# Diffusion-trunk step on one Trainium2 core: score matmuls of a head's two maps issued in turn, pass by pass

## The reference

```python
def diff_attention(q, k, v, lam):
    ...
        s = jnp.einsum('bqhsd,bkhsd->bshqk', qblk.astype(jnp.float32), kf) * scale
        p = jax.nn.softmax(s, axis=-1)
        a = p[:, 0] - lam * p[:, 1]
        return jnp.einsum('bhqk,bkhv->bqhv', a, vf)
```

## Time and profile before

| | |
|---|---|
| median of 3 runs | 2035.17 us (2033.72 to 2036.74) |
| span of the profiled execution | 2036.0 us |
| PE busy | 1926.5 us, 95% of the span |
| DVE busy | 1603.3 us, 79% |
| ACT busy | 1164.4 us, 57% |
| attention stage | about 524 to 720 us of the span |
| DMA queue q1, packet time | 68.5% of 16 engines over the span |

### The profile page before, as it was taken

How to read it: one execution, slowest core, us unless ns; L and a number is a source line. 1 busy time by engine, 2 the same in 40 slices (tenths; PEclk the granted TensorE clock), 3 DMA queues, 4 the chain that set the end, 5 groups by cost and what they waited for, 6 DMA issues and landing times.

```text
span 2036.0 us, 25353 instructions
## 1 busy us (share of the span) xinstructions
PE 1926.5 (95%) x9008; PEld 1373.6 (67%) x9008; DVE 1603.3 (79%) x1588; ACT 1164.4 (57%) x1190; POOL 151.9 (7%) x130
## 2 busy tenths in 40 slices
PE   4899999999789887799999999999999999999998
PEld 2787777877677766566666666666666666666665
DVE  4599437333577756679999999999999999999997
ACT  5444324232477722167667666767676776766764
POOL 0265203000011110000000000000000000000000
PEclk8899999999799998799999999999999999999999
DMA  8233634433222120299999999999999999999996
GB/s 295 99 114 140 232 125 134 159 115 124 79 63 82 44 94 31 102 319 366 343 352 354 348 347 347 357 339 347 354 347 347 347 355 344 350 350 342 351 355 219
DMA packets 270387, 504.50 MB, mean 248 GB/s; under 512 B 11372, under 2 KB 37268, under 8 KB 270328
## 3 DMA queue, kind: packets, MB, share of 16 engines
q1 hardware_dynamic: 266648, 491.10, 68.5%
q0 software_dynamic: 3680, 12.60, 1.7%
HBM read 486.86 MB, written 16.80 MB: 247 GB/s over the span
## 4 chain that ended last, share of the span: by engine, by line
PE 83%; DVE 6%; POOL 3%; DMA 2%; ACT 2%; SPq 2%; issue 1%; DVEq 0%; ACTq 0%; POOLq 0%
PE banks L1454 23%; PE banks L1456 23%; PE banks L1455 23%; PE banks L1730 2%; PE banks L1616 2%; PE banks L1731 2%; POOL qk_swp L1381 2%; POOL qk_swp L1376 1%; DMA v_h<-v_scr 1%; PE banks L1473 1%; PE banks L1474 1%; DVE w_lo L912 1%; PE banks L1588 1%; PE banks L1718 1%; PE banks L1701 1%
## 5 line engine op out<-in xcount | busy, mean ns | idle before, releaser
L1342 DVE TENSOR_TENSOR w_lo<-raw,w_hi 128x2048 fp32r<-128x2048 f32 x285 | 649.9, 2285 | 71.2 <-ACT w_hi L889 70.3
L889 ACT ACTIVATE w_hi<-raw 128x2048 fp32r<-128x2048 f32 x285 | 546.0, 1916 | 129.4 <-PE banks L1456 113.9
L1454 PE MATMUL banks<-w_hi,xe_hi 128*80 128x512 f32 x1024 | 404.9, 395 | 2.6 <-issue 2.6
L1456 PE MATMUL banks<-w_lo,xe_hi 128*80 128x512 f32 x1024 | 402.9, 393 | 0.0
L1455 PE MATMUL banks<-w_hi,xe_lo 128*80 128x512 f32 x1024 | 402.4, 393 | 0.0
L889 ACT ACTIVATE w_hi<-raw_x 128x2048 fp32r<-128x2048 f32 x96 | 184.3, 1920 | 153.7 <-PE banks L1456 106.5
L1454 PE MATMUL banks<-w_hi,h_hi 128*128 128x512 f32 x560 | 223.5, 399 | 2.0 <-POOL h_lo L1368 1.0
L1342 DVE TENSOR_TENSOR w_lo<-raw_x,w_hi 128x2048 fp32r<-128x2048 f32 x96 | 218.9, 2280 | 5.4 <-ACT w_hi L889 5.3
L1455 PE MATMUL banks<-w_hi,h_lo 128*128 128x512 f32 x560 | 221.7, 396 | 0.0
L1456 PE MATMUL banks<-w_lo,h_hi 128*128 128x512 f32 x560 | 221.7, 396 | 0.0
L1456 PEld LDWEIGHTS banks<-w_lo,xe_hi 128*80 128x80 f32 x1024 | 151.2, 148 | 85.1 <-issue 0.5
(11 more groups left out here) (208 smaller groups left out, 2505.4 us busy)
## 6 DMA issues: line engine op xcount, KB each, us to landing
raw<-in_w_gate_e SPq DMA_DIRECT2D x128, 1024.0 KB, 5.1
raw<-in_w_down_e SPq DMA_DIRECT2D x96, 1024.0 KB, 5.1
raw<-in_w_up_e SPq DMA_DIRECT2D x64, 1024.0 KB, 5.5
raw_x<-in_w_up_e SPq DMA_DIRECT2D x64, 1024.0 KB, 5.4
raw_x<-in_w_down_e SPq DMA_DIRECT2D x32, 1024.0 KB, 5.2
raw<-in_w_in SPq DMA_DIRECT2D x28, 1024.0 KB, 5.6
raw<-in_w_ada SPq DMA_DIRECT2D x24, 1024.0 KB, 5.9
raw<-in_w_out SPq DMA_DIRECT2D x4, 1024.0 KB, 5.3
```

The costliest lines, as they stand in the source:

```text
L889: nc.scalar.activation(w_hi[:, j % NSPLIT], raw_slot(slot), ACT.Copy).then_inc(hi_done, 1)
L1342: nc.vector.tensor_tensor(w_lo[:, j % NSPLIT], raw_slot(EXPERT_SLOT[j % NRAWE]), w_hi[:, j % NSPLIT], ALU.subtract).then_inc(lo_done, 1)
L1454: nc.tensor.matmul(ps, hi, wh, start=first, stop=False)
L1456: return nc.tensor.matmul(ps, hi, wl, start=False, stop=last)
```

## The change

The waits for both maps now stand ahead of the first score matmul of a unit. The matmuls are issued pass by pass: high by high of map 0, then of map 1, low by high of map 0, then of map 1, and so on, at 512 columns and then at 256. The number, shapes, operands and banks of the matmuls are the same. Each map's `sc_done` is raised by its own last matmul. No other engine's program changes. The score matmuls have line L1608 now, and `weigh` L1620.

```diff
                 for s in range(2):
                     if u >= 1:
                         pe.wait_ge(exp_done[s], u)
-                    d, c = slice(HD * s, HD * s + HD), slice(t * P, (t + 1) * P)
-                    for b, w in ((0, min(nk, 4) * P), (1, (nk - 4) * P)):
-                        if w > 0:
-                            k = slice(k0 * P + b * CW, k0 * P + b * CW + w)
-                            last = split3(bank(2 * s + b)[:, 0:w], qT_hi[d, h % 2, c], qT_lo[h % 2][d, c],
-                                          kT_hi[d, h % 2, k], kT_lo[d, h % 2, k], True, True)
-                    last.then_inc(sc_done[s], 1)
+                c = slice(t * P, (t + 1) * P)
+                for b, w in ((0, min(nk, 4) * P), (1, (nk - 4) * P)):
+                    if w > 0:
+                        k = slice(k0 * P + b * CW, k0 * P + b * CW + w)
+                        for n, (q, kk) in enumerate(((qT_hi[:, h % 2, c], kT_hi[:, h % 2, k]), (qT_lo[h % 2][:, c], kT_hi[:, h % 2, k]),
+                                                     (qT_hi[:, h % 2, c], kT_lo[:, h % 2, k]))):
+                            for s in range(2):
+                                d = slice(HD * s, HD * s + HD)
+                                last = nc.tensor.matmul(bank(2 * s + b)[:, 0:w], q[d], kk[d], start=(n == 0), stop=(n == 2))
+                                if n == 2 and (b == 1 or nk <= 4):
+                                    last.then_inc(sc_done[s], 1)
```

## The result

| | before | after |
|---|---|---|
| median of 4 runs each, same chip | 2035.07 us (2033.72 to 2036.74) | 2051.59 us (2049.13 to 2055.45) |
| ratio, 95% interval | | 1.0082 (1.0065 to 1.0099) |
| span of the profiled execution | 2036.0 us | 2051.8 us (a run of 2053.71) |
| first scores of head 0 to t = 4 of head 7 | 183.56 us | 202.73 us |

The change made the kernel 16.5 us slower. The attention stage took 19.2 us more in the profiled execution, 5.0 less passed ahead of it (the first scores start at 519.84 instead of 524.81, in code that is the same), and 1.6 more behind it: 15.8 between the two spans. A second profile of each kernel gave 203.13 and 184.58 us for the stage, and the unchanged kernel started it at 518.07. So the 5 us ahead of the stage are the run's own and no gain of the change, and the stage costs 18.2 to 19.6 more.

The account below looks back on a forecast made before the run. PE looked like the limit, but overlapping maps set the pace; the new wait makes it the 4.63 us way round. 9.3 + 2.6 + 1.1 + 1.3 = 14.3 on 2036.0 gives 2050.3, less 0.8 for the median: 2049.5, range 2045 to 2060.

Parts of the forecast that it names:

- The term, the wait for `exp_done1` ahead of map 0: Latent units: each starts only after the previous unit's map 1 exponential; start to start becomes 4.63 us, from 3.69 and 3.58.
- Its handshake: Between ACT's accumulator end for map 1 and PE's next matmul: 655.24 to 655.30, within the 4.63 us pace.
- One head: Attention heads 1 to 7, first scores to next head's: 23.09 us becomes 24.64, or 9.3 us over six heads.
- The clock term: PE clock dips in the six heads: two dips as before, 0.65 us each, adding 1.3 us.
- The rival in which the clock falls: PE idling in latent units halves its clock in ten to twenty of 32; 10 to 20 us, 2060 to 2070; chance 0.12.
- The ends: Head 7 up to t = 3 takes 2.6 us more; head 0, largely at half clock, takes 1.1 us more.
- PE idle ahead of a unit: Expected sign in latent units: PE idle up to 1 us before each, released by ACT's map 1 exponential.
- Matmuls at nothing: Score matmuls: 432 before and after, same shapes; map 0's scores still ready 1.35 us behind their start, so cost 0.
- The rival of pairs that take turns: On PE's array the two maps alternate, so map 0's scores come up to 1 us later, 32 times: 2080; chance 0.03.
- The sign "within some 0.01 us of each other": Expected in the profile after: score matmuls of both maps start within some 0.01 us of each other.
- PE's saving at nothing: PE's score stretch, about 0.6 us shorter, hardly helps `weigh`, which also waits for ACT's copies and outputs.
- PE is the bound: Rival for the attention stage: shorter score stretches start units sooner, down to 3.58 us; 4 us faster, 2031; chance 0.03.

## Why the prediction was right

It said 2049.5 us in 2045 to 2060, slower with 0.95; measured were 2051.59 and, again, 2050.50. By its steps:

- **The term, the wait for `exp_done1` ahead of map 0**: right. The order of the passes left as it was, the moved wait alone makes the pace 4.69. The size was 4.63, measured 4.69 and 4.72.
- **Its handshake was mis-sized.** The 0.06 us from rows 3 and 4 (655.24 to 655.30) held for one wait. With two ahead of the matmul it is 0.15, and the kernel with one wait went back to 0.06 and to 4.63. In six heads this is 6 x (24.79 - 24.64) = 0.9 us.
- **One head**: 24.64 against 24.79 where the clock did not fall. Within it, t = 3 to the transposes of the next queries was put at 5.20 and measured 5.08 (616.14 to 621.22 in head 3), and their releaser is ACT's copy at L785 instead of the loads, as said. From there to the next scores it was 5.60, put at 5.55.
- **The clock term was mis-sized**: 1.3 us put in, 153.9 - 6 x 24.79 = 5.2 measured in one profile and 152.5 - 148.7 = 3.8 in the other. The prediction took two dips as before. In the changed kernel the clock fell in five heads of six: ahead of or at the first scores of t = 3 in heads 1, 2 and 5, and shortly behind them in heads 4 and 6. PE's gaps are longest ahead of t = 3 (up to 2.30 us), but head 3, which has no fall, has that gap too. The stretch of the first fall, after:

```profile
563.40:570.30 6.90, 6.32 (x30) 5.63 (x30) 4.27 (x8) 4.08 (x12) 0.46 (x1) 0.51 0.51 147
```

  Its granted clock is 0.51, that is 1.2 GHz, for 6.9 us, and the unit's maximum starts 2.29 behind S. The rival in which the clock falls had ten to twenty latent units at half; in the six heads it was three whole ones and parts of two (maxima 1.42 and 1.82 behind S). So it came in small. By the number of dips the prediction's own bound "every head with a dip, 2054" was the nearer one; the measured time lies between it and the 2049.5.

  By the Trainium skill, "TensorE: Matmul & The Clock Gate", section HAM oscillation, gaps as short as these, taken one by one, would leave the clock alone; the row above does not agree with that for this kernel, whose longest gap ahead of it was 2.30 us. The kernel with work in the gap, at 0.97, points the same way. That the gap is the cause is not shown beyond this, since the kernel with the waits moved had shorter gaps and the lowest clock of the three.
- **The ends**: head 7 from its first scores to t = 4 went from 15.96 to 18.79, 2.8 for 2.6. Head 0 went from 29.07 to 30.05, 1.0 for 1.1 (29.34 and 30.90 in the second profiles, 1.6).
- **PE idle ahead of a unit**: put at up to 1 us, measured 1.21 ahead of t = 1, 1.64 ahead of t = 2 and 2.30 ahead of t = 3. The 0.94 of the later start and the 0.6 that the score stretch no longer fills, which the prediction left out here, add up to 1.54 of the 1.64.
- **Matmuls at nothing**: right. The maximum starts 1.32 to 1.35 behind S at full clock, and 2.25 if both maps use the same rows. The rival of pairs that take turns is out by that. The sign "within some 0.01 us of each other" held for the first pair of a unit; the others are up to 0.04 apart in units that waited.
- **PE's saving at nothing**: right at full clock. At half clock it is worth about 1 us a unit at t = 3, which the prediction did not say.
- **Sum**: 15.4 (six heads, 9.3 + 0.9 + 5.2) + 2.8 + 1.0 = 19.2 in the stage, where it had 14.3. Medians differ by 16.5, between the two, with an interval of 13 to 20. That the forecast came within 2.1 us of the median is in part luck: by the profiles it had 4 to 5 us too little in the stage, the clock and the second wait above all, and the runs differ by less than the stages. Its lower bound has a slip: with no dips and a first head at 1.0 its own terms give 9.3 + 2.6 + 1.0 over 2035.2, that is 2048.1 and not 2047. The stated range does not hang on it.
- **PE is the bound**: out. It was right that a unit can start 3.57 behind the last; it needs a unit in front whose exponentials are done, which only t = 0 has, and the next unit gives it back.

## What to carry to other kernels

Before merging two streams that run half a turn apart, find which buffer each waits for. Issued in turn, both wait for the later one; the loss is the distance of the two releases for each unit in which that wait decides (here 0.94 of 3.69 us), and it comes whatever the matmuls gain. A busy share of 89% on PE did not make it the bound: only the timeline of one unit, followed from its start to the release of each bank, told that. Run a moved wait alone, without the new order, as the first experiment: one kernel separates the two.

## What the runs showed of the hardware

- A second semaphore wait ahead of a matmul that stands waiting lengthened the time from ACT's last event to the matmul from 0.06 to 0.15 us (657.23 to 657.29, and 661.34 to 661.49).
- A pair of passes on rows 0-63 and 64-127 costs the time of one here. In the unit at 656.80 the third pair of passes starts at 657.34, 0.54 behind; before, map 0's third pass started 0.57 behind its first with no partner. Nor did the old order need help to overlap: map 1's first pass, the seventh in program order, starts at 651.29, ahead of map 0's fourth at 651.47. With both on rows 0-63 the whole stretch up to the maximum grew from 1.32 to 2.25 us.
- The granted clock was 0.87 over the six heads of the kernel whose PE was busy for 130.5 of 159.4 us (82%), and 0.95 over those of the kernel with one wait, busy for 107.2 of 149.6 (72%):

```profile
548.50:698.10 149.60, 107.23 (x849) 89.84 (x848) 103.32 (x235) 100.79 (x288) 22.71 (x36) 0.95 0.23 64
```

The busier PE had the lower clock (part of the 82% is the half clock itself), so the busy share of a stretch doesn't foretell it.
